# A 32-expert MoE tail whose weight loads for experts 5 and 6 wait for the first gather of token rows

## The chip, the cores and the metric

One Trainium2 chip, one core of it. The time is the device time of one execution in microseconds; where several runs are given, their median. A profile is one further execution, recorded by the hardware profiler, and all stage times below are counted from the start of its span.

## The reference

One inference step of a single-layer decoder trunk, 512 prompt tokens and 8 sample tokens, width 1024, float32 throughout. After a token mixer (a combined input projection, a gated branch, an RWKV-7 branch, an output projection), the part that matters here is the mixture of experts: 32 experts in 4 groups, each token goes to the top 2 experts of its top group.

```
grp = argmax(x2d @ router_group + bias)
le_g = (x2d @ router_expert + bias)[:, grp]          # 8 experts of the group
top_v, top_i = lax.top_k(le_g, 2)
for e in range(32):
    h = silu(x2d @ moe_w_gate[e]) * (x2d @ moe_w_up[e])   # 1024 -> 256
    y = y + combine[:, e:e + 1] * (h @ moe_w_down[e])      # 256 -> 1024
x = x + y;  y_out = RMSNorm(x)
```

Each expert has three weight matrices of 1 MiB (gate, up, down), 96 MiB for all 32, and every expert's weights are read once from DRAM.

## The kernel before

Everything around the change is in `phase_tail`, in which each engine runs its own instruction list, written out by hand, and waits for the others on semaphores.

**Tokens.** TensorE (PE) ends the output projection in four row tiles (`out_part`, L2344), counted by semaphore `s_o`. The normalised token rows of each tile are stored to the DRAM tensor `d_tok` from the ACT queue (`store`, L2568), beside a copy of the residual in `d_x2` (L2569, in the profile `d_x<-tl_x`), which raises `s_keep`. The router then runs on PE and DVE and ends in lists of token numbers for each expert, `ex_gidx`. Semaphore `s_list` tells POOL that they are ready.

**Gathers.** POOL gathers the token rows of a pair of experts with one indirect DMA (`gather(p)`, L2293, `tl_xn<-d_tok,ex_gidx`); 64 slots belong to each expert, and slots without a token are skipped. There are two buffers, with semaphores `s_in[0]` and `s_in[1]`, each raised by 16 when a gather into it has landed. `gather(0)` and `gather(1)` are issued at once, `gather(2)` when PE has turned the first pair (`s_t`).

**Experts.** For expert k, PE does `gate_up` (L2464, `tl_psA<-...`), then, when k is even, turns the next pair (`turn_pair`, L2456), then does `down` of expert k-1 (L2474, `psv<-...`) and turns the hidden rows (L2469). `gate_up` of k waits for the slot semaphore `m.s_gate_up[k % 7]`, `down` for `m.s_down[k % 8]`. After expert 31 there is one pass for the tokens of experts with more than 64, with weights loaded once more, and then the results are read back from `d_y`, combined, normalised and stored.

**Weights.** The SP queue issues all weight loads in order. `load_gate_up(x, k)` is two DMAs of 1 MiB (L2087) into one of seven slots, `load_down` one of 1 MiB (L2093) into one of eight. In the profile a slot has the name of the memory it lies in: `xT`, `bonus_all`, `r_all`, `w_expert`, `w_lo`, `mg`, `spare` for gate and up of k % 7 = 0 to 6, so experts 5 and 6 are loaded as `mg<-in_moe_w_gate` and so on and as `spare<-...`. The down matrices of experts 4 and 5 lie in `tl_x`, that of 6 in `tl_xnT`. Slots 4, 5 and 6 come free only when the output projection is over. SP's list in this place is:

```
eng.wait_ge(s_o, NT)             # output projection over
load_gate_up(eng, m, a, 5, 5)
load_gate_up(eng, m, a, 6, 6)
eng.wait_ge(s_r, 3)
eng.wait_ge(s_sq, NTT)
load_down(eng, m, a, 6, 6)
for j in range(2, NT):
    eng.wait_ge(s_keep[j], 16)
eng.wait_ge(s_xn, NTT)
load_down(eng, m, a, 5, 5)
for k in range(SLOTS, NE):       # 7 to 31
    eng.wait_ge(s_gu, k - SLOTS + 1)
```

`s_gu` counts the finished `gate_up`s, so expert 7 is requested when the `gate_up` of expert 0 is over, and so on.

Of the kernel before, what the change touches and what calls it, by code (L numbers as in the profile page):

```python
# [2083 lines left out]
def load_gate_up(eng, m, a, x, expert):  # L2084

    for n, src in enumerate((a["moe_w_gate"], a["moe_w_up"])):
        eng.dma_start(m.wgu[x][:, n], src[0, bass.ds(expert, 1)].rearrange("a (p k) f -> p (a k) f", p=P))\  # L2087
           .then_inc(m.s_gate_up[x], 16)


def load_down(eng, m, a, x, expert):

    eng.dma_start(m.wd[x][:, :, :], a["moe_w_down"][0, bass.ds(expert, 1)].rearrange("a (k p) c -> p (a k) c", p=P))\  # L2093
       .then_inc(m.s_down[x], 16)
# [6 lines left out]
def phase_tail(nc, m, a):  # L2101
# [4 lines left out]
    with ctx:  # L2106
# [90 lines left out]
        s_in = [sem(f"e_x{n}") for n in range(2)]  # L2197
# [19 lines left out]
        def passes(eng):  # L2217
            eng.wait_ge(s_passes, 1)
            return eng.value_load(m.passes[0:1, 0:1], min_val=1, max_val=EXTRA)

        @code.sync
        def _(eng):
            for j in range(NT):
                eng.dma_start(x2w[:, j, :], a["x_prompt"][0, j * P:(j + 1) * P, :]).then_inc(s_x[j], 16)
            eng.dma_start(x2s[0:TS, :], a["x_sample"][:, 0, :]).then_inc(s_x[NT], 16)
            for x in range(4):
                load_gate_up(eng, m, a, x, x)
                load_down(eng, m, a, x, x)
            load_down(eng, m, a, DOWNS - 1, DOWNS - 1)
            eng.wait_ge(s_t2, nth_of[1])  # L2230
            for j in range(2):
                eng.wait_ge(s_keep[j], 16)
            eng.wait_ge(s_xn, nth_of[1])
            load_down(eng, m, a, 4, 4)
            eng.wait_ge(s_lo, 1)
            load_gate_up(eng, m, a, 4, 4)
            eng.wait_ge(s_o, NT)
            load_gate_up(eng, m, a, 5, 5)
            load_gate_up(eng, m, a, 6, 6)
            eng.wait_ge(s_r, 3)  # L2240
# [6 lines that stand above are left out]
            for k in range(SLOTS, NE):  # L2247
                eng.wait_ge(s_gu, k - SLOTS + 1)
                load_gate_up(eng, m, a, k % SLOTS, k)
                if k >= DOWNS:  # L2250
                    eng.wait_ge(s_down, k - DOWNS + 1)
                    load_down(eng, m, a, k % DOWNS, k)
            n = passes(eng)
            with eng.Fori(0, n) as q:
                e = eng.value_load(m.block_expert[0:1, bass.ds(q, 1)], min_val=0, max_val=NE - 1)
                eng.wait_ge(s_gu_free, q + 1)
                load_gate_up(eng, m, a, SPARE, e)
                eng.wait_ge(s_d_free, q + 1)
                load_down(eng, m, a, SPARE_D, e)
            eng.wait_ge(s_gu, 26)  # L2260
            eng.wait_ge(s_down, 30)
            for j in range(NT):
                eng.dma_start(fx[:, j, :], m.d_x2[j * P:(j + 1) * P, :]).then_inc(s_fx, 16)
            eng.dma_start(fxs, m.d_x2[TP:T, :]).then_inc(s_fx, 16)
            eng.dma_start(gf[:, :], a["norm_final_w"].partition_broadcast(P)).then_inc(s_fx, 16)
            eng.wait_ge(s_y[0], n * 16 + NE // 2 * 16)
            eng.wait_ge(s_y[1], NE // 2 * 16)
            rows = m.d_y2.rearrange("(c t h) d -> t c (h d)", c=2, h=2)
            eng.dma_start(fys[0:TS, :, :], rows[TP:T]).then_inc(s_fy[NT], 16)
            for j in range(NT):  # L2270
                eng.dma_start(fy[j // 2][:, j % 2, :, :], rows[j * P:(j + 1) * P]).then_inc(s_fy[j], 16)
            for i, j in enumerate(final):
                eng.wait_ge(s_fo, i + 1)
                if j < NT:
                    eng.dma_start(a["y_prompt"][0, j * P:(j + 1) * P, :], fx[:, j, :]).then_inc(s_out, 16)
                else:
                    eng.dma_start(a["y_sample"][:, 0, :], fxs).then_inc(s_out, 16)
            eng.wait_ge(s_out, 16 * NTT)
# [803 lines left out]
```

## Time and profile before

| | |
|---|---|
| median of 3 runs | 1109.95 us (1108.62 to 1112.37) |
| profiled execution | 1114.5 us, of which the span 1112.8 us |
| PE busy | 1014.0 us, 91% of the span |
| DVE, ACT, POOL busy | 51%, 33%, 40% |
| moved by DMA | 183.11 MB, mean 165 GB/s |
| mean granted clock of TensorE | 0.973 of full |

The profile cuts the span into 40 slices of 27.8 us and gives for each the busy share of each engine and of the 16 DMA engines. The tail begins near 758 us (slice 27), the first expert near 848 us, the last pass ends near 1079 us. A "landing" is the time from the issue of a DMA to the end of its transfer. Idle time of PE ahead of a `gate_up` that waits for weights is shown as "issue" in the timeline, since the semaphore was raised by a DMA.

### The profile page before, as it was taken

What the parts mean: (1) busy time and instruction counts of PE and PEld (TensorE: products, weight loads), DVE (VectorE), ACT (ScalarE), POOL (GpSimd) and SP (SyncE); (2) the same over time, 40 slices, a digit from 0 to 9 for tenths busy, and PEclk for the clock granted to TensorE, in tenths of its full rate; (3) what the DMA queues carried; (4) which work ended last, traced back from release to release, by engine and by line L of the source; (5) the groups of instructions that cost most, each with busy time, mean ns of one, the idle gap of its engine ahead of it and who ended that gap; (6) DMA issues with size and microseconds to landing.
All of it is one profiled execution on the core that took longest, in us unless ns stands there. A gap on an engine that the chain in (4) does not pass through costs nothing. (4 is left out here: it accounts for less than half of the span.)

```text
span 1112.8 us, 24781 instructions
## 1 busy us (share of the span) xinstructions
PE 1014.0 (91%) x10429; PEld 766.1 (69%) x10429; DVE 564.1 (51%) x1195; ACT 364.7 (33%) x783; POOL 442.7 (40%) x458
## 2 busy tenths in 40 slices
PE   5999999789989999999999999999976999988883
PEld 4777777578878887888888888884554555554441
DVE  5587678656555643777645446324362322211126
ACT  3444544545545443444344451000111111111111
POOL 7646546244654424877663335410001222221110
PEclk9999999899999999999999999999986999999897
DMA  8122121110000007541242214407976999999965
GB/s 257 32 79 70 58 81 38 42 43 4 4 4 4 4 4 185 166 113 39 56 145 91 76 53 174 151 2 273 372 294 253 416 414 416 415 417 416 416 276 227
DMA packets 84935, 183.11 MB, mean 165 GB/s; under 512 B 9921, under 2 KB 59613, under 8 KB 76122
## 3 DMA queue, kind: packets, MB, share of 16 engines
q1 hardware_dynamic: 78173, 168.59, 41.6%
q0 software_dynamic: 5168, 8.56, 2.1%
q10 hardware_dynamic: 1485, 4.39, 1.0%
q8 instruction: 83, 1.36, 0.5%
q14 instruction: 26, 0.21, 0.1%
HBM read 173.24 MB, written 17.55 MB: 171 GB/s over the span
## 5 line engine op out<-in xcount | busy, mean ns | idle before, releaser
L2298 POOL DMA_INDIRECT d_y<-tl_xn,ex_sidx x32 | 31.9, 996 | 121.1 <-DVE tl_xn L2810 110.9
L2806 DVE SCALAR_TENSOR_TENSOR ex_sg<-tl_psA,ex_slot_rs,ex_sg 128x128 f32<-128x128 f32 x32 | 11.2, 351 | 134.2 <-ACT ex_sg L2606 134.1
L2293 POOL DMA_INDIRECT tl_xn<-d_tok,ex_gidx x17 | 17.8, 1048 | 143.7 <-DVEq L2798 78.1
L264 PE MATMUL psv<-xT,w_sum 128*128 128x260 f32 x256 | 61.6, 384 | 1.1 <-DVE uv_gu L1597 0.6
L226 POOL TENSOR_TENSOR w_sum<-w 128x512 f32<-128x512 f32 x16 | 21.2, 1324 | 94.1 <-PE mg_w L264 93.8
L264 PEld LDWEIGHTS psv<-xT,w_sum 128*128 128x128 f32 x256 | 48.4, 190 | 9.6 <-issue 1.0
L2606 ACT ACTIVATE ex_sg<-tl_psA,ex_slot_rs 128x128 f32<-128x128 f32 x32 | 11.7, 367 | 126.8 <-PE tl_psA L2464 126.8
L1060 PE MATMUL ck_b<-ck_X,ck_V 64*64 64x64 f32 x1280 | 50.4, 222 | 3.2 <-issue 2.1
L264 PE MATMUL rk_ps<-xT,rk_w 128*128 128x260 f32 x208 | 50.1, 384 | 0.0
L264 PE MATMUL rk_ps<-xS,rk_w 128*128 128x260 f32 x200 | 48.6, 386 | 0.0
L1060 PEld LDWEIGHTS ck_b<-ck_X,ck_V 64*64 64x64 f32 x1280 | 43.0, 134 | 4.4 <-issue 4.1
L1059 PE MATMUL ck_b<-ck_V,ck_X 64*64 64x64 f32 x1024 | 39.9, 221 | 4.9 <-DVE ck_V L1254 3.4
L264 PEld LDWEIGHTS rk_ps<-xT,rk_w 128*128 128x128 f32 x208 | 39.3, 190 | 6.7 <-issue 0.8
L264 PEld LDWEIGHTS rk_ps<-xS,rk_w 128*128 128x128 f32 x200 | 37.4, 190 | 8.0 <-issue 2.5
L1254 DVE TENSOR_TENSOR ck_V<-psv,levels 128x256 f32<-128x256 f32 x40 | 16.8, 420 | 48.1 <-PE psv L1041 48.1
L1059 PEld LDWEIGHTS ck_b<-ck_V,ck_X 64*64 64x64 f32 x1024 | 34.7, 134 | 9.4 <-issue 7.9
L2810 DVE COPY tl_xn<-psv 128x512 f32<-128x512 f32 x33 | 22.8, 691 | 34.5 <-PE psv L2474 34.5
L1187 ACT ACTIVATE ck_Z<-ck_b 128x256 f32<-128x256 f32 x64 | 24.4, 381 | 46.6 <-PE ck_b L1059 44.4
L982 POOL TENSOR_TENSOR ck_bk<-br_all,ck_pi 64x512 f32<-64x512 f32 x14 | 17.8, 1269 | 40.8 <-ACT ck_pi L1153 40.3
L264 PE MATMUL uv_psw<-xS,w_uv 128*128 128x260 f32 x128 | 30.7, 383 | 1.2 <-PEq L123 1.2
L264 PE MATMUL psv<-xT,w_uv 128*128 128x260 f32 x128 | 31.3, 387 | 0.0
L264 PE MATMUL psv<-xT,w 128*128 128x260 f32 x128 | 30.9, 384 | 0.0
(617 smaller groups left out, 2789.4 us busy)
## 6 DMA issues: line engine op xcount, KB each, us to landing
wd<-in_moe_w_down SPq DMA_DIRECT2D x13, 1024.0 KB, 23.7
rk_w<-in_w_in SPq DMA_DIRECT2D x12, 1024.0 KB, 5.4
w_uv<-in_w_in SPq DMA_DIRECT2D x16, 512.0 KB, 5.2
w<-in_w_in SPq DMA_DIRECT2D x8, 1024.0 KB, 5.8
tl_x<-in_moe_w_down SPq DMA_DIRECT2D x8, 1024.0 KB, 21.7
xT<-in_moe_w_gate SPq DMA_DIRECT2D x5, 1024.0 KB, 16.9
xT<-in_moe_w_up SPq DMA_DIRECT2D x5, 1024.0 KB, 19.5
bonus_all<-in_moe_w_gate SPq DMA_DIRECT2D x5, 1024.0 KB, 19.5
```

Of the source, the lines that this page charges most:

```text
L226: eng.tensor_tensor(w.t3, w.b22, w.b12, ALU.subtract).then_inc(sem, 1)
L264: ins = eng.matmul(bank[:, 0:TH], w[:, k, :], x[:, k, :], start=(first and k == 0), stop=(last and k == NK // 2 - 1), skip_group_check=True)
L982: eng.tensor_tensor(bk[rows, :, rows], m.br[rows, :, at], pi[rows, :, :], ALU.mult).then_inc(s_bk, 1)
L1059: new_z = eng.matmul(b64(bank[g][2])[own, n, :], X[at, p, :], V[at, p, :], start=True, stop=True)
L1060: new_x = eng.matmul(b64(bank[g][3])[other, n, :], V[at, p, :], X[at, p, :], start=True, stop=True)
L1187: eng.activation(Z[:, grp(g), :], b64(bank[g][2]), ACT.Copy).then_inc(s_z_e[g], 1)
L1254: eng.tensor_tensor(V[:, grp(g), :], b64(bank[g][1]), m.levels[:, lv + 1, :].unsqueeze(1).to_broadcast([P, GP, CH]), ALU.mult)\
L2293: eng.indirect_dma_start(out=xg[:, p % 2, :], out_offset=None, in_=m.d_tok, in_offset=bass.IndirectOffsetOnAxis(ap=gidx[:, p:p + 1], axis= ...
L2298: eng.indirect_dma_start(out=m.d_y2, out_offset=bass.IndirectOffsetOnAxis(ap=rows, axis=0), in_=yo[:, x, :], in_offset=None, bounds_check= ...
L2606: eng.activation(sg[:, out, :], psg[out][:, 0:P], ACT.Silu, scale=scale).then_inc(s_sg, 1)
L2806: eng.scalar_tensor_tensor(out=sg[:, out, :], in0=psg[out][:, P:2 * P], scalar=scale, in1=sg[:, out, :], op0=ALU.mult, op1=ALU.mult).then_ ...
L2810: eng.tensor_copy(yo[:, out, :], psd[out]).then_inc(s_yo, 1)
```

## The change

One wait is put on SP's list, between the wait for the output projection and the four loads of experts 5 and 6: SP now goes on only when `s_in[0]` is at least 16, that is when `gather(0)` has landed.

```
             load_gate_up(eng, m, a, 4, 4)
             eng.wait_ge(s_o, NT)
+            eng.wait_ge(s_in[0], 16)
             load_gate_up(eng, m, a, 5, 5)
             load_gate_up(eng, m, a, 6, 6)
             eng.wait_ge(s_r, 3)
```

On SP, at the end of the first loads of the tail, the place looks as follows (minus is before, plus is after; the name in brackets is that of the first phase that used the physical semaphore: `r_decay` stands for `s_o`, `t_ident` for `s_in[0]`).

```order
 L2087 DMA w_lo<-in_moe_w_gate 128x2048 [waits r_rate]
 L2087 DMA w_lo<-in_moe_w_up 128x2048
-L2087 DMA mg<-in_moe_w_gate 128x2048 [waits r_decay]
+L2087 DMA mg<-in_moe_w_gate 128x2048 [waits t_ident,r_decay]
 L2087 DMA mg<-in_moe_w_up 128x2048
 L2087 DMA spare<-in_moe_w_gate 128x2048
```

Nothing has moved: the first load of expert 5 has one semaphore more to wait for. Behind it SP's list is the same in both kernels; the next rows, here of the changed kernel, are those that now stand behind the new wait too.

```order
L2087 DMA spare<-in_moe_w_up 128x2048
L2093 DMA tl_xnT<-in_moe_w_down 128x2x1024 [waits r_kk2,r_rn]
L2093 DMA tl_x<-in_moe_w_down 128x2x1024 [waits r_ss,r_zw,r_mixed]
L2087 DMA xT<-in_moe_w_gate 128x2048 [waits l_in]
L2087 DMA xT<-in_moe_w_up 128x2048
L2087 DMA bonus_all<-in_moe_w_gate 128x2048 [waits l_in]
L2087 DMA bonus_all<-in_moe_w_up 128x2048
```

These are the down matrices of experts 6 and 5 and the first loads of experts 7 and 8. The other engines have the same instructions as before, in the same order.

## Rows read from the trace of the kernel before

**Rows 1.** The page, busy tenths of PE and DMA in 40 slices.

```profile
PE   5999999789989999999999999999976999988883
...
DMA  8122121110000007541242214407976999999965
```

**Rows 2.** PE timeline, late experts: start, us, instruction, idle before it.

```profile
981.72 3.67 PE L2464 MATMUL tl_psA<-xT,tl_xn 128*64 128x256 f32 x32 [1.17 <-issue]
...
990.30 5.36 PE L2464 MATMUL tl_psA<-bonus_all,tl_xn 128*64 128x256 f32 x32 [2.94 <-issue]
...
1064.15 3.67 PE L2464 MATMUL tl_psA<-w_expert,tl_xn 128*64 128x256 f32 x32 [1.46 <-issue]
```

**Rows 3.** SP's queue: start and length of DMA issues.

```profile
822.93 0.33 SPq L2087 DMA_DIRECT2D mg<-in_moe_w_gate  x1
...
853.25 0.34 SPq L2087 DMA_DIRECT2D xT<-in_moe_w_gate  x1
...
1039.56 3.11 SPq L2087 DMA_DIRECT2D w_expert<-in_moe_w_up  x1
```

**Rows 4.** DMA issues at 1039.5 to 1040 us: size, us to landing.

```profile
w_expert<-in_moe_w_up SPq DMA_DIRECT2D x1, 1024.0 KB, 24.5
```

**Rows 5.** Busy time by stretch, with clock, DMA share, GB/s.

```profile
823.00:825.00 2.00, 2.00 (x27) 1.74 (x28) 1.96 (x2) 0.69 (x1) 0.00 (x0) 1.00 0.60 111
823.00:854.00 31.00, 16.05 (x126) 12.19 (x126) 12.51 (x52) 5.13 (x9) 3.25 (x3) 0.67 0.70 260
854.00:856.00 2.00, 0.76 (x6) 0.34 (x5) 0.93 (x3) 1.60 (x4) 0.93 (x1) 1.00 0.77 229
862.00:1062.00 200.00, 186.27 (x1344) 103.53 (x1340) 44.46 (x90) 27.36 (x72) 42.51 (x42) 0.97 1.02 415
...
845.00:855.00 10.00, 8.45 (x48) 5.35 (x48) 1.30 (x5) 2.28 (x4) 0.99 (x1) 0.67 0.20 47
```

**Rows 6.** The chain that ended last, 838 to 853 us.

```profile
838.20 6.58 DMA tl_xn<-d_tok,ex_gidx
...
844.91 1.96 PE tl_psT L2456 x8
...
847.64 5.60 PE tl_psA L2464 x32
```

**Rows 7.** DMA queues and issues, 823 to 854 us: MB and share, us to landing.

```profile
q1 hardware_dynamic: 1120, 6.29, 54.3%
q10 hardware_dynamic: 288, 1.05, 8.3%
q0 software_dynamic: 432, 0.69, 7.6%
...
spare<-in_moe_w_up SPq DMA_DIRECT2D x1, 1024.0 KB, 14.2
tl_xnT<-in_moe_w_down SPq DMA_DIRECT2D x1, 1024.0 KB, 12.2
```

**Rows 8.** POOL timeline, the second and third gather.

```profile
839.78 0.99 POOL L2293 DMA_INDIRECT tl_xn<-d_tok,ex_gidx  x1 [0.31 <-issue]
847.62 0.99 POOL L2293 DMA_INDIRECT tl_xn<-d_tok,ex_gidx  x1 [6.86 <-PE tl_psT L2456]
```

**Rows 9.** Line L2293, its 17 gathers: us from start to landing.

```profile
DMA to landing us min/median/max: 4.0/8.0/10.0
```

**Rows 10.** DMA issues at 847 to 848 us.

```profile
tl_xn<-d_tok,ex_gidx POOLq DMA_INDIRECT x1, 4.0
```

**Rows 11.** PE timeline, first uses of what is moved.

```profile
864.92 1.09 PE L2456 MATMUL tl_psT<-ident,tl_xn 128*128 128x128 f32 x8
...
881.81 3.67 PE L2464 MATMUL tl_psA<-mg,tl_xn 128*64 128x256 f32 x32
...
894.14 3.67 PE L2464 MATMUL tl_psA<-xT,tl_xn 128*64 128x256 f32 x32
```

More of the change, by code:

```diff
@@ L2237, in _ @@
             eng.wait_ge(s_o, NT)
+            eng.wait_ge(s_in[0], 16)
             load_gate_up(eng, m, a, 5, 5)
```

## The prediction

> **What bounds the kernel now.** I began with the slices of the page: PE is at 9 tenths nearly everywhere and falls to 8 near the end, while the DMA row stands at 9 in all late slices [rows 1]. A busy DMA next to a PE with holes says that the end may belong to the weights. The timeline of PE decides it. From 981.72 us on, PE stops ahead of a `gate_up` several times: 1.17 us, 2.94 us and, ahead of expert 31, the last, 1.46 us [rows 2]. That last one I followed to its load: the up matrix of expert 31 is issued at 1039.56 [rows 3] and lands 24.5 us later [rows 4], at 1064.06; PE starts at 1064.15 [rows 2]. So there is 0.09 us between landing and use, and all that follows (expert 31, the extra pass, the final sum) hangs on this landing. The issue itself took 3.11 us, so SP is pushed back by its full queue; the load does not wait for a slot. The windows close the argument: from 862 to 1062 the DMA engines are at a share of 1.02 and move 415 GB/s in the mean [rows 5]. From about 854 us on the weights are one unbroken stream. Its end is fixed by when it starts and how many bytes are ahead of it. Whatever DMA time is left empty before 854 and has to be made up after it moves the end.
>
> Then I looked at the stretch that the change touches. PE, at half clock and idle, waits for `gather(0)`: start 838.20, landing 6.58 us later, PE goes on at 844.91 [rows 6]. Beside it run the loads of experts 5 and 6, issued from 822.93 [rows 3]; the last of the four landed after 14.2 us [rows 7], at about 838.5, and the down matrix of expert 6 (`tl_xnT`) was behind them. When PE works on expert 0, DMA is nearly empty: share 0.20 from 845 to 855 [rows 5]. SP has nothing that it may ask for until `gate_up` of expert 0 frees a slot, at 853.25 [rows 3].
>
> **What the change does.** It adds no instruction that takes engine time; it makes the four loads start after the landing of `gather(0)` and holds back everything behind them on SP: the down matrices of 6 and 5, then expert 7. Step by step:
>
> *The gather.* No wait ahead of it changes, so it starts at 838.20 as before; the chain from the router is arithmetic. What landing will it have on an empty DMA? Over all 17 gathers the landing is 4.0 at least, 8.0 in the median [rows 9]; the one of 4.0 is the third, started at 847.62 [rows 8, 10], in the empty stretch. I take 4.0, landing at 842.20; the bounds are 4.0 and 6.58. PE then starts its first pair 2.6 us earlier (844.91 to 842.3).
>
> The Trainium skill ("DMA: Bandwidth & Descriptors", anatomy of one DMA on the SWDGE path) fits such a DMA as about 2.0 us plus bytes by 436 GB/s, an estimate of 2.5 us for 0.23 MB. By it the landing would be at 840.7, the loads would start 1.5 us sooner, and the time would be 1113.7. The trace's lowest landing, 4.0, is well above it; the measured one decides, and the sum goes by that.
>
> *The loads.* SP sees the landing some 0.13 us later (as PE did, 844.78 to 844.91 [rows 6]), so the first load goes out at 842.35. Before, the first went out at 822.93, and by 825 it and its followers had moved 2 us x 111 GB/s = 0.22 MB [rows 5], which at 415 GB/s is 0.53 us: the stream began in effect at 824.47, 1.54 us after its issue. So in the changed kernel it begins at 843.9.
>
> *What it must carry before expert 7.* Between 823 and 854 the kernel moves 31 us x 260 GB/s = 8.06 MB [rows 5]: 6.29 MB of weights (six loads), 1.05 MB of stores on the ACT queue, 0.69 MB in three gathers [rows 7]. The stores and the first gather (0.23 MB) will be over by 842.2. 8.06 - 1.05 - 0.23 = 6.78 MB remain, at 415 GB/s 16.3 us, so expert 7's turn comes at 843.9 + 16.3 = 860.2.
>
> *Against before.* There the bytes of expert 7 began in effect at 856 - 2 x 229 / 415 = 854.9 [rows 5]. The stream is late by 860.2 - 854.9 = **5.3 us**. Put otherwise, some 18 us of DMA between 824.5 and 842 now stand nearly empty but for the stores, and the empty 8 us of 845 to 855 (10 us at share 0.20) win back only part.
>
> *Bounds.* Below: the two later gathers slip between the loads and cost nothing (0.46 MB, 1.1 us less), and the last small hole at 855 to 862 goes (some 0.4 us): 3.8 us. Above: before, the six loads took 54.3% of 31 us = 16.8 us of DMA time [rows 7] against 15.2 at 415 GB/s, 1.6 us more; and if the gather still takes 6.58 us, 2.6 us more: 6.9 and 7.9, together 9.5.
>
> *What it does not cost.* Expert 5's weights are first used at 881.81 [rows 11], 2.6 us sooner in the changed kernel, and land before about 853. Expert 7's are used at 894.14 [rows 11] and would land near 867. The issues behind the wait (six, 0.4 to 0.6 us each) are over by about 845.5, and `gate_up` of expert 0 ends at 850.7 at the earliest, so SP is not late for expert 7. The second gather starts at 839.78 [rows 8], ahead of the loads. The third, at about 845.0, has the loads beside it; PE wants it at 864.92 - 2.6 = 862.3 [rows 11]. Even if it had to stand behind all 6.78 MB it would land by 860.2. So no new stall stands between 842 and the late experts; without that cover the worst would be a few us, which PE's waits from 981.72 on would take up.
>
> *Where the 2.6 us go.* PE is earlier by 2.6 us from the first pair to about expert 18, then it meets a stream that is 5.3 us later. PE's waits in the late experts grow by 5.3 + 2.6 = 7.9 us in all. At expert 31 only the landing counts: 1064.1 + 5.3 = 1069.4.
>
> **The sum.** Gain at the first gather 2.6 us, worth nothing at the end; loss at the end 5.3 us. The profiled execution, 1114.5 us, becomes 1119.8. It stands 4.5 us above the median of the runs, 1109.95; I put the same difference on the median: 1109.95 + 5.3 = **1115.2**.
>
> **The rivals.**
>
> *PE sets the end* (faster). Then the early gather is worth its 2.6 us and the late stream nothing: 1107.3. For it: PE is busy 9 tenths and the profiled run is slower than the median, so in others the weights may come with more room. Against it: the load of expert 31 would have to land 7.9 us ahead of its use, and it has 0.09. Chance 0.05.
>
> *The stream makes up most of it* (no change). Less than 3.3 us late, which is 0.3% and about what a measurement of this kernel can tell from none: the lower bound of 3.8 with a median that falls a little low; the three runs of before lie 3.7 us apart. About 1112.5. Against it: there is no empty DMA time between 862 and 1062 in which to catch up. Chance 0.13.
>
> *The gather is no faster, or the loads go as slowly as before* (slower still). 6.9 to 7.9 us, 1117.4. For it: the landing of 4.0 is one single row, of a gather that did not read rows just stored. Against it: the first gather had 415 GB/s of loads beside it. Chance 0.12.
>
> *The clock falls at the end* (slower still). After the wait of 2.94 us `gate_up` takes 5.36 us in place of the 3.67 that it takes after waits of 1.17 and 1.46 [rows 2]. Where the wait ahead of expert 31 grows to that length, 1.7 us are added behind the last landing: 1116.9. Against it: PE will be equally late with expert 30, and two landings stay as far apart as they were. Chance 0.08.
>
> *The change does as forecast*: 0.62, with a range of its own of 1113.7 to 1117.0. That it does nothing at all is left out: the four issues stand at 822.93, long before 842.2.
>
> **How the numbers follow.** Slower by over 0.3% takes in the forecast and the last two rivals, 0.82; no change 0.13; faster 0.05. The range of 1112.0 to 1118.4 holds the forecast, most of the no-change case and most of the slower ones; both bounds together and the faster case are left out.
>
> **What the profile would show.** The load `mg<-in_moe_w_gate` is issued at 842 to 843, not 822.93. The first gather lands in 4 to 4.5 us and PE turns the first pair at about 842.3. DMA is nearly empty from about 830 to 842 but for the gathers, and full from 845 without a break to the end of the weights. PE's first wait for weights comes about three experts sooner, near 950 to 960. Expert 31's `gate_up` begins near 1069.4. I am wrong if that start moves by less than 3 us, or if PE waits for the third gather or for weights near 860 to 900; if it moves as said and the time does not, then the tail behind it hides the loss.

## The result, and the profile after

| | before | changed |
|---|---|---|
| median | 1112.29 us (1108.62 to 1118.3, 14 runs) | 1116.39 us (1113.94 to 1119.81, 14 runs) |
| ratio | | 1.0037, 95% interval 1.0024 to 1.005 |
| profiled execution | 1114.5 us, span 1112.8 | 1117.33 us, span 1115.6 |

The change makes the kernel slower by 0.37%, 4.1 us on the medians.

SP's queue after the change, start and length of each issue:

```profile
840.51 0.33 SPq L2087 DMA_DIRECT2D mg<-in_moe_w_gate  x1
...
849.05 0.34 SPq L2087 DMA_DIRECT2D xT<-in_moe_w_gate  x1
...
1043.24 3.10 SPq L2087 DMA_DIRECT2D w_expert<-in_moe_w_up  x1
```

The first load of expert 5 has moved from 822.93 [rows 3] to 840.51. The chain that ended last (the sequence of work in which each piece waited for the one before it) shows why it is not later, and what PE has from it:

```profile
836.84 3.60 DMA tl_xn<-d_tok,ex_gidx
...
840.58 1.95 PE tl_psT L2457 x8
...
843.30 5.73 PE tl_psA L2465 x32
```

The first gather lands in 3.60 us where it took 6.58 [rows 6]. Line numbers behind the change are higher by one. In this execution the gather itself started at 836.84, not 838.20. That difference arose ahead of the new wait: expert 4's down matrix was already issued 3.2 us sooner (806.61 against 809.77), and the stretch from there to the gather was 1.8 us longer, for a reason that the last section shows. So times near the gather are best read from its start: the first load of expert 7 is asked for 12.21 us after it (before, 853.25 - 838.20 = 15.05).

Busy time by stretch (length, busy us of PE, PE's loads, DVE, ACT and POOL, then clock, DMA share, GB/s):

```profile
828.00:838.00 10.00, 2.82 (x28) 2.37 (x28) 6.05 (x33) 0.32 (x2) 1.16 (x1) 0.50 0.02 9
845.00:855.00 10.00, 8.76 (x67) 5.47 (x65) 3.34 (x10) 2.41 (x4) 0.99 (x1) 0.88 1.01 420
862.00:1062.00 200.00, 178.73 (x1280) 100.18 (x1278) 39.57 (x77) 25.88 (x69) 41.49 (x41) 0.97 1.02 415
```

DMA is idle ahead of the gather (share 0.02), and the hole behind it, share 0.20 in [rows 5], is filled (1.01). In the 200 us from 862 on it moves 415 GB/s, exactly as before. PE in the late experts:

```profile
958.92 3.67 PE L2465 MATMUL tl_psA<-w_lo,tl_xn 128*64 128x256 f32 x32 [1.66 <-issue]
...
1043.78 3.67 PE L2465 MATMUL tl_psA<-xT,tl_xn 128*64 128x256 f32 x32 [2.42 <-issue]
...
1067.80 3.67 PE L2465 MATMUL tl_psA<-w_expert,tl_xn 128*64 128x256 f32 x32 [1.13 <-issue]
```

The first wait for weights is at expert 18 (958.92) where it was at expert 21 (981.72 [rows 2]), and expert 31 starts at 1067.80 where it started at 1064.15. From the start of the gather that is 230.96 us against 225.95, 5.0 us more. PE's waits for weights ahead of a `gate_up` add up to 22.4 us in this profile, 15.2 before.

### The profile page after: what moved, and what is told of

The parts are those of the page before. It is cut to its first block and busy times, and to the rows that moved or that the text cites. A ratio compares the mean times of both kernels' runs of the same rounds, so it can differ in the third digit from the quotient of the medians.

```text
span 1115.6 us, 24782 instructions
## 1 busy us (share of the span) xinstructions
PE 1017.0 (91%) x10429; PEld 770.4 (69%) x10429; DVE 565.8 (51%) x1195; ACT 365.0 (33%) x783; POOL 442.3 (40%) x458
## 3 DMA queue, kind: packets, MB, share of 16 engines
q8 instruction: 83, 1.36, 0.5%
## 5 line engine op out<-in xcount | busy, mean ns | idle before, releaser
L2607 ACT ACTIVATE ex_sg<-tl_psA,ex_slot_rs 128x128 f32<-128x128 f32 x32 | 11.8, 367 | 134.6 <-PE tl_psA L2465 134.6
```

## The experiments

Each was timed beside the kernel before, run again on the same chip (median there 1112.18 us for experiments 1 to 4, 1113.24 us for 5 to 7). The ratio is to that kernel, with a 95% interval in brackets. Beside it I read one time from each profile that does not depend on what came ahead of the tail: the start of `gate_up` of expert 28, where PE waited for weights in all of these kernels but those of experiments 3 and 4, counted from the start of the first gather. Before it is 1040.21 - 838.20 = 202.0 us, after the change 1043.78 - 836.84 = 206.9 us, 4.9 more. There is one profile of each run; how well such a reading repeats is seen in experiment 7.

**1. The wait ends at the token lists, not at the landing.** A delay nearly as long, but 4.6 us shorter.

```
-            eng.wait_ge(s_in[0], 16)
+            eng.wait_ge(s_list, 1)
```

> The loads of experts 5 and 6 wait for the token lists (s_list, some 14 us after the projection's end and at the start of the first gather) in place of the gather's landing (18 us). Stream theory: only what the stream of weights still has to carry when expert 7 may be asked for is lost. Issued at about 837.3, in effect moving from 838.8, with 8.06 - 1.05 = 7.0 MB ahead of expert 7, 16.9 us, so expert 7's turn comes at 855.7 against 854.9: +0.8 us, within 0.1% of before. The first gather lands in about 6.6 us as before, since it has loads beside it. Rival, loss in proportion to the delay: 14.4 of 17.6 us of delay, 0.82 of the measured 4.1 us: +3.4 us, 0.3% slower.

Measured: ratio 1.0014 (0.9992 to 1.0036). The first load of expert 5 went out 0.93 us ahead of the gather. POOL's gather, PE's first turn and the first and a late `gate_up` in this kernel:

```profile
836.70 1.27 POOL L2294 DMA_INDIRECT tl_xn<-d_tok,ex_gidx  x1 [76.38 <-DVEq L2799]
...
845.01 1.94 PE L2457 MATMUL tl_psT<-ident,tl_xn 128*128 128x128 f32 x8 [7.75 <-DMA tl_xn<-d_tok,ex_gidx]
...
847.73 6.63 PE L2465 MATMUL tl_psA<-xT,tl_xn 128*64 128x256 f32 x32 [0.78 <-DVE tl_xn L2804]
...
1041.12 5.36 PE L2465 MATMUL tl_psA<-xT,tl_xn 128*64 128x256 f32 x32 [2.46 <-issue]
```

The ratio lies between the two expectations (1.0007 and 1.003) and its interval holds both; the profile tells more. Expert 28 starts 1041.12 - 836.70 = 204.4 us after the gather, 2.4 more than before, not 0.8. What I had wrong was the gather: it started with the loads and landed 8.2 us after its start, not 6.6. Then the first `gate_up` took 6.63 us in place of 5.60 [rows 6], since the granted clock stayed at half for longer (0.50 from 848 to 853; before, 0.65). So expert 7 was asked for at 17.7 us from the gather's start and not at 15.05: 2.65 us later, 1.6 of it by the gather and the rest by the clock, and that accounts for the 2.4. The backlog cost nothing here, a late request did: between 854 and 855 DMA was at a share of 0.31, so the loads held back were over before the bytes of expert 7 began. The rival, a loss in proportion to the delay (+3.4), is not far from the 2.4; what speaks against it is this gap and, with more weight, experiment 6.

**2. Only expert 6 waits.** Expert 5 is loaded at once, both down matrices too, and 2.1 MB stand behind the wait.

```
             load_gate_up(eng, m, a, 5, 5)
-            load_gate_up(eng, m, a, 6, 6)
             eng.wait_ge(s_r, 3)
             eng.wait_ge(s_sq, NTT)
             load_down(eng, m, a, 6, 6)
...
             load_down(eng, m, a, 5, 5)
+            eng.wait_ge(s_in[0], 16)
+            load_gate_up(eng, m, a, 6, 6)
             for k in range(SLOTS, NE):
```

> Expert 5's two loads go out at once as before, then the down matrices of 6 and 5, and only the two loads of expert 6 (2.1 MB) wait for the first gather. Stream theory: the gather finds DMA empty, lands in 3.6 to 4.0 us and PE is 2.6 to 3.0 us sooner; the 2.1 MB are over by about 849, before expert 7 may be asked for at about 850.5, so nothing is lost and the stream starts 2.6 to 3.0 us sooner than before: ratio 0.9973 to 0.9977, the end earlier by that. Rival, PE's early start is worth nothing because the stream sets the end: no change. Rival, any wait of a load on the gather costs: slower by 1 to 2 us.

Measured: 1107.85 us, ratio 0.9967 (0.9951 to 0.9983), faster than both kernels. POOL, PE and SP in its profile:

```profile
836.01 1.27 POOL L2294 DMA_INDIRECT tl_xn<-d_tok,ex_gidx  x1 [78.05 <-DVEq L2799]
...
839.73 1.94 PE L2457 MATMUL tl_psT<-ident,tl_xn 128*128 128x128 f32 x8 [3.16 <-DMA tl_xn<-d_tok,ex_gidx]
...
847.70 0.33 SPq L2087 DMA_DIRECT2D xT<-in_moe_w_gate  x1
...
1034.44 3.67 PE L2465 MATMUL tl_psA<-xT,tl_xn 128*64 128x256 f32 x32 [2.86 <-issue]
```

The gather has the same short landing (3.6 us) as in the changed kernel; expert 7 is asked for 11.69 us after the gather's start, 3.4 us sooner than before and with nothing ahead of it, and expert 28 starts at 198.4 us, 3.6 less than before. In these kernels PE's early start is worth something when it lets the next load be asked for sooner while DMA is free.

**3 and 4. The stream out of the way.** The same cut in both kernels: of the gate and up loads of experts 12 to 31 only an eighth of the bytes is fetched, and these experts are computed with what lies in their slots from earlier loads, so only the times are of use.

```
+def load_thin(eng, m, a, x, expert):
+    for n, src in enumerate((a["moe_w_gate"], a["moe_w_up"])):
+        rows = src[0, bass.ds(expert, 1)].rearrange("a (p k) f -> p (a k) f", p=P)
+        eng.dma_start(m.wgu[x][:, n, 0:1, :], rows[:, 0:1, :]).then_inc(m.s_gate_up[x], 16)
...
-                load_gate_up(eng, m, a, k % SLOTS, k)
+                (load_thin if k >= 12 else load_gate_up)(eng, m, a, k % SLOTS, k)
```

> The kernel before, but the gate and up loads of experts 12 to 31 bring only one of eight parts of their bytes (experts 12 to 31 are computed with stale weights), so the stream cannot set the end. Stream theory: PE's waits ahead of the late experts (about 15 us) and the low clock behind them (about 6 us) go: some 20 us less than before, near 0.982. Compared with the same cut of the changed kernel: see there. Rival, PE sets the end already: 0 to 2 us less.

> The changed kernel with the same cut (experts 12 to 31 get only one of eight parts of their gate and up bytes and are computed with stale weights). Stream theory: with the stream out of the way only the early landing of the first gather is left, so it is 2.6 to 3.0 us faster than the cut kernel of before. Rival, the added wait costs something else on the way (a late third gather, expert 5 or 7 late, SP late): no gain, or slower than the cut kernel of before.

Measured, against the kernel before: the cut kernel of before 1092.33 us, ratio 0.982 (0.9791 to 0.9848); the cut kernel of the change 1087.78 us, ratio 0.9785 (0.9755 to 0.9815). The first is the expectation to the digit: the end was set by the stream, and that cost 20 us, PE's waits and the slower matmuls behind them together. The second is ahead of the first by 4.5 us, more than the 2.6 to 3.0 expected. All five of its runs (1086.11 to 1090.55) are below all five of the other (1090.57 to 1094.46), so the sign is clear; the two intervals, each 6 us wide, overlap, so the size is not. Their profiles have gathers landing in 6.4 and 3.6 us, 2.8 apart. The first `gate_up` gives 0.7 of that back (5.91 and 6.60 us), and expert 31 starts 204.13 and 201.98 us after the gather's start: 2.15 us sooner, the worth of the early landing that the profiles show. The span ends at 255.0 and 251.1 us; the further 1.8 us lie behind the start of expert 31, and nothing here says why. In both PE is busy without a gap from 862 to 1032 us, here in the cut kernel of the change:

```profile
862.00:1032.00 170.00, 170.00 (x1274) 91.63 (x1272) 38.63 (x75) 25.43 (x68) 40.58 (x41) 1.00 0.80 289
```

**5. The wait made longer still.** The loads wait for the first `gate_up`.

```
-            eng.wait_ge(s_in[0], 16)
+            eng.wait_ge(s_gu, 1)
```

> The four loads wait for the gate and up products of expert 0 (s_gu) in place of the gather's landing: in the changed kernel that is 8.5 us later. By then DMA has been empty since the third gather and nothing is left to win back. Stream theory, counted from the start of the first gather: the loads in effect move at 12.2 + 1.5 = 13.7 us, carry 6.3 to 6.5 MB at 415 GB/s, 15.2 to 15.7 us, so expert 7's turn comes at 29.0 to 29.4 us against 16.7 before: 12.3 to 12.7 us slower, ratio 1.0111 to 1.0114. The gather keeps its short landing. Rival, what costs in the changed kernel is the waiting on a landing as such or the gather's neighbours: 4 to 5 us slower, as there.

Measured: 1123.84 us, ratio 1.0099 (1.0078 to 1.012), 10.6 us slower on the medians. The gather still lands in 3.6 us. SP's queue and expert 28 (the gather started at 834.30):

```profile
846.09 0.33 SPq L2087 DMA_DIRECT2D mg<-in_moe_w_gate  x1
...
849.18 0.47 SPq L2087 DMA_DIRECT2D xT<-in_moe_w_gate  x1
...
1047.95 5.36 PE L2465 MATMUL tl_psA<-xT,tl_xn 128*64 128x256 f32 x32 [2.40 <-issue]
```

Expert 28 starts 213.65 us after the gather, 11.6 more than before; 12.3 to 12.7 were expected. Most of a further delay is lost once hardly any hole is left to take it back: the loads went out 11.79 us after the gather's start, 8.1 us later than in the changed kernel, and expert 28 is 6.7 us later than there.

**6. The down matrices ahead of the wait.** 4.2 MB behind it in place of 6.3.

```
-            load_gate_up(eng, m, a, 5, 5)
-            load_gate_up(eng, m, a, 6, 6)
             eng.wait_ge(s_r, 3)
...
             load_down(eng, m, a, 5, 5)
+            eng.wait_ge(s_in[0], 16)
+            load_gate_up(eng, m, a, 5, 5)
+            load_gate_up(eng, m, a, 6, 6)
             for k in range(SLOTS, NE):
```

> Both experts' gate and up loads (4.2 MB) wait for the gather as in the changed kernel, but the two down matrices (2.1 MB) are issued ahead of the wait. Stream theory, counted from the start of the first gather: the loads in effect move at 3.7 + 1.5 = 5.2 us, carry 4.19 + 0.46 MB, 11.2 us, so expert 7's turn comes at 16.4 us against 16.7 before: no change, -0.3 us, ratio 0.9997. It lies between the changed kernel (6.3 MB behind the wait, +4.1 us) and the kernel in which only expert 6 waits (2.1 MB, -3.7 us measured). Rival, the wait costs through experts 5 and 6 themselves: +4 us as in the changed kernel.

Measured: ratio 1.0006 (0.9988 to 1.0025), no change. Experts 5 and 6 are as late as in the changed kernel (their first load 3.61 us after the gather's start, there 3.67), so their lateness costs 0.8 us at most in itself, and the loss of the changed kernel does not go with the delay of these loads. Expert 28 starts at 1042.07 - 839.30 = 202.8 us, 0.8 more than before. The row:

```profile
1042.07 5.02 PE L2465 MATMUL tl_psA<-xT,tl_xn 128*64 128x256 f32 x32 [3.12 <-issue]
```

**7. Experiment 2 again**, since 0.3% is little.

> The kernel in which only expert 6's two loads (2.1 MB) wait for the gather, once more, to see whether its lead over before holds on other runs. Stream theory: expert 7's turn is set by its request, 13.3 us from the start of the gather against 16.7: 3.4 us faster, ratio 0.997. Rival: the first measurement was scatter, no change.

Measured: 1108.07 us, ratio 0.9961 (0.9945 to 0.9976). The lead holds. Its profile is a second one of the same kernel:

```profile
1031.22 3.67 PE L2465 MATMUL tl_psA<-xT,tl_xn 128*64 128x256 f32 x32 [2.92 <-issue]
```

The gather started at 832.89, so expert 28 starts 198.33 us after it, where the first profile had 198.43. Counted from the gather, the reading repeats within 0.1 us.

Side by side:

| kernel | MB behind the wait | expert 7 asked for, us from gather | expert 28 against before | last load issued, against before | ratio |
|---|---|---|---|---|---|
| only expert 6 waits | 2.1 | 11.69 | -3.6 | -3.4 | 0.9967, 0.9961 |
| down matrices ahead | 4.2 | 12.38 | +0.8 | +0.8 | 1.0006 |
| before | none | 15.05 | 0 | 0 | 1 |
| waits for the lists | 6.3 | 17.7 | +2.4 | +2.6 | 1.0014 |
| the change | 6.3 | 12.21 | +4.9 | +5.0 | 1.0037 |
| waits for `gate_up` 0 | 6.3 | 14.88 | +11.6 | +11.8 | 1.0099 |

The last column but one is read off SP's queue, independently of PE: the issue of the up matrix of expert 31 (1043.24 after the change, 1039.56 before), counted from the gather.

One rule fits every row: the long stream of expert 7 and its followers starts either when it is asked for or when the bytes ahead of it are gone, whichever is later, and the end moves with it. Worked out with the 1.5 to 1.65 us from issue to moving bytes, 415 GB/s and the gathers counted among the bytes, it gives -3.4, -0.3, 0, +2.7, +4.8 and +12.1 us for the six rows, each within 1.2 us of what was read; the largest miss, 1.1 us in the row of the down matrices, has no explanation here. For the list wait the late request was put in after the run; for the three last experiments the rule's figures stood in the expectations.

## Why the prediction was right

*The bound.* That the end hangs on the stream of weights was argued from one landing 0.09 us ahead of its use and from a full DMA; the cut kernel showed it, 20 us less with seven eighths of the late gate and up bytes gone, and DMA moves 415 GB/s over the same 200 us in both kernels. PE's waits for weights grew by 7.2 us (15.2 to 22.4), where the forecast had 7.9.

*The gather.* It was to land 4.0 us after its start, between bounds of 4.0 and 6.58. It landed after 3.60, and again after 3.6 in all five later kernels in which the loads stood behind it. The bound from a single row was 0.4 us too high. The Trainium skill's fit ("DMA: Bandwidth & Descriptors", anatomy of one DMA on the SWDGE path), an estimate of 2.5 us, was further off than the row.

*The loss at the end.* Forecast 5.3 us; by the profiles 4.9 at expert 28 and 5.0 at expert 31, by the medians 4.1 (2.7 to 5.6 by the interval). The oversized term is this landing: with 3.6 in place of 4.0 the sum gives 4.9. The rest of the difference to the median is inside its interval. That the forecast time, 1115.2, lies so near the 1116.39 measured is in part luck: the three runs behind it had the kernel before at 1109.95, the fourteen runs at 1112.29, and this 2.3 us too little was half made up by the 1.2 us too much in the loss. The profiled execution came out at 1117.3 in place of 1119.8, because that execution had its gather 1.36 us sooner, its last part, from expert 31 to the end of the span, 0.85 us shorter (47.8 against 48.65), and a loss of 5.0 in place of 5.3.

*What was to cost nothing.* PE has no wait for weights before 958.92 and none at the third gather (its pair, the third, is turned at 860.72 without a gap). Experiment 6 shows apart that late loads of experts 5 and 6 cost 0.8 us at most; experiment 2 that the wait on the landing is free.

*Where the gain went.* The forecast gave PE's early start no worth at the end. In the changed kernel that is so, and experiments 3 and 4 give what it is worth at expert 31 once the stream is out of the way, 2.15 us. But the forecast held only because 6.3 MB stood in front of expert 7. With 2.1 MB there the same early start was worth 3.6 us: through the earlier request, not through PE's own work. The forecast named the earlier `gate_up` of expert 0 only as an absence of harm; it did not draw this out.

*The rivals.* That PE sets the end is refuted by the result itself (PE 3.0 us earlier, the kernel slower) and by experiments 3 and 5; experiment 2, which is faster, would by itself fit that rival too. That the stream makes up the loss is refuted by the full DMA windows and by the last load, issued 5.0 us later. A slow gather was wrong here, but it is what happened in experiment 1. The clock rival did not come true in the changed kernel: ahead of expert 31 PE waited 1.13 us, and its `gate_up` took 3.67 us. But its mechanism is real. In experiment 6 PE waited ahead of expert 30, whose `gate_up` then took 5.36 us (granted clock 0.62 and 0.52 in 1058 to 1060 and 1060 to 1062, 1.00 behind it). The last landing was at 1041.41 + 24.5 = 1065.9, PE began expert 31 without a wait at 1066.65, and so the low clock cost about 0.7 us. No run was made to force the larger loss that the forecast named.

## What to carry to other kernels

Where a long stream of transfers sets the end, as here, look for the empty DMA time ahead of it, and ask of each hole whether something behind it can still fill it. In this kernel a wait that clears the way for one urgent transfer was free for as many bytes as fitted between that transfer and the next request: 2.1 MB gained, 4.2 MB came out even and 6.3 MB lost. And ask what an early start of the compute engine frees: here it was the slot for the next load.

## What the runs showed that I had not expected

The time from the issue of expert 4's down matrix to the start of the first gather, a stretch with the same instructions in every kernel, has three values: 26.7 us (four profiles), 28.4 (two) and 30.1 to 30.3 (three), the kernel before among the middle ones and the changed kernel among the long ones. It goes with TensorE's granted clock: in the four profiles with 26.7 us the clock is full over the first 13.5 us of that stretch, in the two with 28.4 it is at half for less than 4 us, and in the three with 30.1 to 30.3 for less than 7. In the kernel before, ahead of the last part of the output projection:

```profile
806.00:814.00 8.00, 8.00 (x53) 6.17 (x51) 5.20 (x22) 1.09 (x2) 0.00 (x0) 1.00 0.60 199
814.00:818.00 4.00, 4.00 (x8) 1.89 (x8) 2.96 (x16) 0.00 (x0) 0.00 (x0) 0.58 1.01 400
```

and in experiment 1:

```profile
806.00:814.00 8.00, 8.00 (x52) 6.07 (x50) 5.39 (x22) 1.09 (x2) 0.00 (x0) 1.00 0.56 197
814.00:818.00 4.00, 4.00 (x13) 2.07 (x13) 2.92 (x16) 0.00 (x0) 0.00 (x0) 1.00 1.04 430
```

PE is busy throughout in both, by the same work, and in one of them the granted clock is 0.58 in the mean of these 4 us (1.00 is 2.4 GHz, the low level of 0.50 is 1.2 GHz): the 16 matmuls of the last projection part take 8.69 us in place of 7.11. Before 814 us both have full clock. The changed kernel has the longer dip, from an earlier point:

```profile
811.00:816.00 5.00, 5.00 (x10) 2.70 (x11) 3.27 (x17) 0.00 (x0) 0.00 (x0) 0.50 1.01 421
```

Which executions have this dip does not follow the kernel (the two profiles of experiments 2 and 7 are of the same kernel and have 28.4 and 26.7 us), and it is worth up to 3.6 us, nearly as much as the change itself. It is one source of the scatter of single runs (10 us from the fastest to the slowest of before). What decides it stays open.
